# A ring layout of its own for the second expert pass, and the last pass's down projection cut into column pieces of 512, 384 and 128

## The reference

```python
def swiglu(h, w_gate, w_up, w_down):
    return (jax.nn.silu(h @ w_gate) * (h @ w_up)) @ w_down

def moe_swiglu(h, w_router, w_gate, w_up, w_down):
    ...
    out = jnp.zeros_like(t)
    for e in range(N_EXPERTS):
        out = out + combine[:, e:e + 1].astype(t.dtype) * swiglu(t, w_gate[e], w_up[e], w_down[e])
    return out.reshape(B, S, D)

# behind both layers
return rms_norm(x, final_norm_g)
```

## Time and profile before

| | us |
|---|---|
| median of 3 runs | 1017.01 |
| lowest, highest | 1016.84, 1018.2 |
| the profiled execution, its own time | 1018.07 |
| its span, first to last instruction | 1016.3 |

### The profile page before, as it was taken

How to read it: one execution, slowest core, us unless ns; L and a number is a source line. 1 busy time by engine, 2 the same in 40 slices (tenths; PEclk the granted TensorE clock), 3 DMA queues, 4 the chain that set the end, 5 groups by cost and what they waited for, 6 DMA issues and landing times.

```text
span 1016.3 us, 22250 instructions
## 1 busy us (share of the span) xinstructions
PE 1001.5 (99%) x9679; PEld 863.3 (85%) x9679; DVE 592.1 (58%) x991; ACT 401.6 (40%) x627; POOL 13.6 (1%) x57
## 2 busy tenths in 40 slices
PE   8999999999999999999999999999999999999995
PEld 8999999999999999999999999996566566566552
DVE  6667766577677565376577665755542542542443
ACT  6735655535544344357356565352102002002012
POOL 3000000000000000000000000000000000000000
PEclk9999999999999999999999999999999999999998
DMA  7453543555555465465435437989979999999993
GB/s 282 160 159 104 198 146 111 187 200 189 176 187 186 144 217 201 150 232 166 163 107 188 154 99 263 394 326 405 405 305 414 410 411 414 413 408 414 414 408 139
DMA packets 56017, 255.40 MB, mean 251 GB/s; under 512 B 6609, under 2 KB 6641, under 8 KB 55922
## 3 DMA queue, kind: packets, MB, share of 16 engines
q1 hardware_dynamic: 55346, 252.94, 67.2%
q10 hardware_dynamic: 576, 1.07, 0.3%
HBM read 252.93 MB, written 1.05 MB: 250 GB/s over the span
## 4 chain that ended last, share of the span: by engine, by line
PE 85%; SPq 9%; DMA 3%; issue 1%; ACT 1%; DVE 1%; DVEq 0%
PE ps L1721 24%; PE ps L1716 18%; PE ps L1717 18%; PE ps L1718 18%; SPq L611 8%; PE ps L1710 2%; PE ps L1711 2%; PE ps L1712 2%; DMA e_ring<-in_experts 2%; DMA raw<-in_dense 1%; PE ps L1926 1%; ACT w_hi L754 0%; ACT squared L759 0%; PE ps L1744 0%; PE ps L1898 0%
## 5 line engine op out<-in xcount | busy, mean ns | idle before, releaser
L1075 DVE TENSOR_TENSOR w_lo<-raw,w_hi 128x1536 fp32r<-128x1536 f32 (+2 forms) x156 | 247.5, 1605 | 122.0 <-ACT w_hi L754 121.6
L754 ACT ACTIVATE w_hi<-raw 128x1536 fp32r<-128x1536 f32 (+2 forms) x156 | 209.2, 1362 | 145.2 <-DMA raw<-in_dense 142.5
L1716 PE MATMUL ps<-hT_hi,w_hi 128*128 128x256 f32 (+1 forms) x816 | 231.7, 284 | 1.6 <-DVE w_lo L1217 1.1
L1717 PE MATMUL ps<-hT_lo,w_hi 128*128 128x256 f32 (+1 forms) x816 | 230.4, 282 | 0.0
L1718 PE MATMUL ps<-hT_hi,w_lo 128*128 128x256 f32 (+1 forms) x816 | 229.6, 281 | 0.0
L1721 PE MATMUL ps<-e_ring,xe 128*32 128x352 f32 (+2 forms) x2480 | 186.5, 459 | 0.0
L1721 PEld LDWEIGHTS ps<-e_ring,xe 128*32 128x32 f32 x2480 | 109.8, 110 | 73.0 <-issue 32.3
L1716 PEld LDWEIGHTS ps<-hT_hi,w_hi 128*128 128x128 f32 (+1 forms) x816 | 152.2, 186 | 5.2 <-issue 2.6
L1717 PEld LDWEIGHTS ps<-hT_lo,w_hi 128*128 128x128 f32 (+1 forms) x816 | 152.3, 187 | 0.4
L1718 PEld LDWEIGHTS ps<-hT_hi,w_lo 128*128 128x128 f32 (+1 forms) x816 | 152.3, 187 | 0.4
L1717 PE MATMUL ps<-h_lo,w_hi 128*128 128x256 f32 x352 | 99.2, 282 | 0.0
(11 more groups left out here) (313 smaller groups left out, 1427.9 us busy)
## 6 DMA issues: line engine op xcount, KB each, us to landing
e_ring<-in_experts SPq DMA_DIRECT2D x124, 704.0 KB, 15.6
raw<-in_dense SPq DMA_DIRECT2D x112, 768.0 KB, 4.3
e_ring<-in_experts SPq DMA_DIRECT2D x88, 512.0 KB, 14.5
raw<-in_dense SPq DMA_DIRECT2D x42, 512.0 KB, 3.5
e_ahead<-in_experts SPq DMA_DIRECT2D x4, 704.0 KB, 9.1
raw<-in_dense SPq DMA_DIRECT2D x3, 544.0 KB, 4.9
raw<-in_dense SPq DMA_DIRECT2D x2, 272.0 KB, 4.2
x<-in_x SPq DMA_DIRECT2D x2, 256.0 KB, 4.5
```

Source lines behind the costliest of these rows:

```text
L754: act.activation(slot(n, "hi", k), slot(n, "raw", k), ACT.Copy).then_inc(hi_done, 1)
L1075: dve.tensor_tensor(slot(n, "lo", k), slot(n, "raw", k), slot(n, "hi", k).bitcast(F32), ALU.subtract).then_inc(lo_done, 1)
L1716: pe.matmul(out, wh, hi, start=first, stop=False, skip_group_check=True)
L1717: pe.matmul(out, wh, lo, start=False, stop=False, skip_group_check=True)
```

## The change

**SP and the ring.** `e_first_place` and `e_first_before` now take the pass as well. Pass 0 keeps its places. Pass 1 has its own: units 0 to 2 go to the columns 0 to 4223 of the ring, which pass 0 leaves with its unit 23, 22 and 21; units 3 and 4 go to `e_ahead`; units 5 to 23 go to where units 0 to 18 were before; from unit 24 on, all have the places of before. The waits are worked out from the overlaps. The loads of pass 2 are written out too, since their waits follow from pass 1's places, and the loop begins at pass 3. The multiplications of passes 0 and 1 read from the new places.

**TensorE, ACT and DVE at the end of the last pass.** The 1024 output columns are cut at 512 and 896. For k = 0 to 7 the right half is multiplied on its first 384 columns only. For k = 8, 9, 10 only the left 512 columns are multiplied as each k lands; then come the overflow of the three, then the 384 columns of the three, then the last 128 columns for k = 0 to 2, then the scatter of the 512 and of the 384 columns, then the last 128 columns for k = 3 to 10, and their scatter. ACT makes `y_hi` of the left half before `weighted_over`; the 384 columns are split into `y_hi` and `y_lo`, as the left half is; DVE makes the last 128 columns (`ehid`) itself. The norm's squares have three pieces.

```diff
-LAST_BANKS = ((2, 3), (0, 1))
+LAST_BANKS = ((2, 3), (0, 1), (5, 7))
...
+LAST_CUT = HALF + 384
+NORM_PIECES = [[], [], [], OCOLS, [(0, HALF), (HALF, LAST_CUT - HALF), (LAST_CUT, D - LAST_CUT)]]
...
+def e_first_place(i, u):
+
+    gate_up, size = 4 * 2 * KQ, 2 * HALF_E
+    shift = len(AHEAD) * size // D
+    if i == 0 and u in AHEAD:
+        return "ahead" + str(AHEAD.index(u) // 2), AHEAD.index(u) % 2 * size, size
+    if i == 0 and 24 <= u < gate_up:
+        return ("ring",) + e_place(u - len(AHEAD))
+    if i == 0 and u >= gate_up:
+        at = CHUNK_AT[0] + size * (gate_up - len(AHEAD) - 24) + D * (u - gate_up)
+        return ("ring",) + ((at, D) if at + D <= CHUNK_AT[0] + CHUNK else e_place(u - shift))
+    spare = shift * D // size
+    if i == 1 and u < spare:
+        return "ring", e_place(len(E_UNITS) - 1)[0] + size * u, size
+    if i == 1 and u < spare + 2:
+        return "ahead0", (u - spare) * size, size
+    if i == 1 and u < 24:
+        return ("ring",) + e_place(u - spare - 2)
+    return ("ring",) + e_place(u)
+
+
+def e_first_before(i, u):
+
+    buffer, at, size = e_first_place(i, u)
+    out = 0
+    for j in range(i + 1):
+        for v in range(u if j == i else len(E_UNITS)):
+            other, a, n = e_first_place(j, v)
+            if buffer == other and a < at + size and at < a + n:
+                out = max(out, j * E_GROUPS + E_GROUP[v] + 1)
+    return out
...
-            for u in range(len(E_UNITS)):
-                sp.wait_ge(e_used, E_GROUP[e_first_before(u)] + 1 if u < 24 else E_GROUPS + E_GROUP[e_before(u)] + 1)
-                expert_load(u, experts)
-            with sp.Fori(2, iters) as i:
+            for i in range(1, 3):
+                experts = [sp.value_load(ids[0:1, 2 * i + e:2 * i + e + 1], min_val=0, max_val=NE - 1) for e in range(2)]
+                for u in range(len(E_UNITS)):
+                    sp.wait_ge(e_used, e_first_before(i, u))
+                    expert_load(u, experts, i)
+            with sp.Fori(3, iters) as i:
...
+            weighted(0)
+            act.wait_ge(y_filled, last * 2 + 2)
             weighted_over()
-            act.wait_ge(y_filled, last * 2 + 2)
-            weighted(0)
             act.wait_ge(y_filled, last * 2 + 3)
-            act.activation(ehid[:, 0:HALF], ps[:, 6, :], ACT.Copy, scale=slot_scale[:, 0:1]).then_inc(y_hi_ready, 1)
...
+            w = LAST_CUT - HALF
+            act.activation(y_hi[:, HALF:LAST_CUT], ps[:, 6, 0:w], ACT.Copy, scale=slot_scale[:, 0:1]).then_inc(y_hi_ready, 1)
...
+            dve.wait_ge(y_hi_ready, last * 4 + 4)
+            rest(1, LAST_CUT - HALF)
+            last_rows(0)
+            last_rows(1)
+            dve.wait_ge(y_filled, last * 2 + 4)
+            dve.tensor_scalar(ehid[:, 0:D - LAST_CUT], ps[:, 4, 0:D - LAST_CUT], slot_scale[:, 0:1], None, ALU.mult).then_inc(last_ready, 1)
+            last_rows(2)
...
-            for q in range(DQ - 1):
-                down(q, last)
-            k = FET - 1
-            down_ready(k, last)
-            down_over([k]).then_inc(y_filled, 1)
-            for h in range(2):
-                down_main(k, h)
...
+            for k in range(late, FET):
+                down_ready(k, last)
+                down_main(k, 0)
+            down_over(range(late, FET)).then_inc(y_filled, 1)
+            for k in range(late, FET):
+                down_main(k, 1, w=w)
...
+            down_last(range(3))
+            pe.wait_ge(y_split, last * 3 + 5)
+            for tt in range(TT):
+                scatter(2 * tt, LAST_BANKS[0][tt])
...
+            pe.wait_ge(y_split, last * 3 + 6)
+            for tt in range(TT):
+                scatter(2 * tt + 1, LAST_BANKS[1][tt], w)
+            down_last(range(3, FET))
+            pe.wait_ge(last_ready, 1)
```

More of the change, by code:

```diff
@@ L532, in load_of, with e_unit @@
             return loaded[n % RING], 16 * (n // RING + 1)
-        def e_unit(u, first=False):
+        def e_unit(u, turn=None):
             _, _, _, k, _, c = E_UNITS[u]
[L537 to L542, removed]
+            buffer, at, size = ("ring",) + e_place(u) if turn is None else e_first_place(turn, u)
+            home = {"ring": e_ring, "ahead0": e_ahead, "ahead1": eb["e_ahead2"]}[buffer]
+            return home[:, at:at + size].rearrange("p (k c) -> p k c", k=k)
         def proj_bank(n):
@@ L641, in _ @@
             for u in free_later["wo"] + AHEAD:
[L642 removed]
+                expert_load(u, (0, 1), 0)
             sp.wait_ge(aux_done, ROUTER_AUX + 1)
@@ L2084, in quads, with hidden @@
                 return ins
-            def hidden(half, q, i, first=False):
+            def hidden(half, q, i, turn=None):
                 u = (half * KQ + q) * 4
-                units = [e_unit(u + n, first) for n in range(4)]
+                units = [e_unit(u + n, turn) for n in range(4)]
                 ks = (2 * q, 2 * q + 1)
@@ L2149, in k_pair, with down @@
                 return range(2 * q, min(2 * q + 2, FET))
-            def down(q, i, first=False):
+            def down(q, i, turn=None):
                 for k in k_pair(q):
@@ L2190, in _, with full_pass @@
             pe.wait_ge(moe_zero, 1)
-            def full_pass(i, first=False):
-                first_half(i, first)
-                second_half(i, first)
+            def full_pass(i, turn=None):
+                first_half(i, turn)
+                second_half(i, turn)
                 for q in range(DQ):
-                    down(q, i, first)
+                    down(q, i, turn)
                 pe.wait_ge(sel_ready, i + 2)
@@ L2226, in _ @@
-            pe.wait_ge(y_hi_ready, last * 4 + 3)
-            for tt in range(TT):
-                out, tokens = last_rows(0, tt)
-                plain(out, selT[:, 0, tokens], y_hi[:, 0:HALF], start=False, stop=False)
+            w = LAST_CUT - HALF
+            late = FET - 3
+            for q in range(late // 2):
+                for k in k_pair(q):
+                    down_ready(k, last)
+                    if k == TURNED:
+                        pe.wait_ge(turn1_read, last * 2 + 1)
+                    down_main(k, 0)
+                    down_main(k, 1, w=w)
+                if q == TURNED // 2:
+                    pe.wait_ge(turn1_read, last * 2 + 2)
+                down_over(k_pair(q))
@@ new lines, in _, with down_last, last_piece @@
+            for k in range(late, FET):
+                down_ready(k, last)
+                down_main(k, 0)
+            down_over(range(late, FET)).then_inc(y_filled, 1)
+            for k in range(late, FET):
+                down_main(k, 1, w=w)
+            def down_last(ks):
+                for k in ks:
+                    down_main(k, 1, LAST_CUT, D - LAST_CUT, 4)
+            def last_piece(tt):
+                return ps[:, LAST_BANKS[2][tt], 0:D - LAST_CUT], slice(tt * P, (tt + 1) * P)
```

111 lines of the change are left out of this document (46 added, 65 removed).

## The result

| | before | changed |
|---|---|---|
| median of 4 runs, us | 1017.17 | 1025.34 |
| lowest, highest | 1016.84, 1018.2 | 1021.64, 1026.02 |
| the profiled execution | 1018.07 | 1021.64 |

The ratio is 1.0071, with a 95% interval of 1.0058 to 1.0083: slower, by more than the range on record allowed. The four executions of the changed kernel took 1021.64, 1025.08, 1025.59 and 1026.02 us, with mean granted clocks of 0.998, 0.996, 0.994 and 0.994. Only the first, which is also the profiled one, lies where the forecast had it. One later execution each of before (1675.8 us), e6 (1311.54) and e9 (5720.59) was in a slow state and is left out of all figures.

A forecast was written before the change was run, and what follows sets the result against it. The prediction took the last down block's landing, T = 1000.2 us, fed by full DMA engines, to set the end. Ring +0.4 and end +3.1 made +3.5 on 1017.0: 1020.5 us, range 1018.8 to 1022.8.

The forecast's parts named there:

- Slower: Whole kernel: time more than 0.2% above the kernel before; chance 0.80.
- the hole: Expert-pass transfers: DMA share lacks 6.5 us at 730 to 750 us; claimed to move from 740 to 782 us, not close.
- Part 2: End of the last pass: from last landing to norm's reduction grows from 9.1 to 12.2 us, +3.1 us.
- Part 1: Pass 1's ring: units 0 to 23 land 6.0 us earlier, the gain is lost, last landing moves by +0.4 us.
- the ring's +0.4: Pass 1's ring: last landing comes 0.4 us later, bounds -0.2 and +0.8.
- the landing of unit 27: Pass 1's ring: unit 27 waits for value 17, at 791.2, and lands at 795.3 us, against 794.9 before.
- rival 3: TensorE at the last down blocks: clock falls to half, work dearer by up to 4 us, 1022 to 1025; chance 0.10.
- Rival 1: Ring's 6.0 us kept: last landing at 994.2, 1014.1 us; decides from where it comes 3.1 us earlier; chance 0.08.
- The 4.5 us put off behind T: Last pass: overflow 0.9, 384 columns 1.3 and 128 columns 2.3 us, formerly done while data came in, follow the last landing.

The follow-up runs named there:

- e6: Kernel before, with pass 1's ring units laid so that none from 24 on waits late, and the old end: 1015.65 us, ratio 0.9986.
- e9: e6 with the places of units 24 and 30 of pass 1 exchanged, so unit 24 waits late again; old end: 1017.8 us, ratio 1.0011.
- e5: Changed kernel with pass 1's units from 24 on laid elsewhere, so that none waits late; new end kept: 1017.46 us, ratio 1.0003.
- e3: Kernel before with only the new end of the last pass, ring unchanged: 1019.82 us, ratio 1.0035.
- e2: Kernel before with only the new ring places of pass 1, old end: 1019.27 us, ratio 1.0024.
- e11: Changed kernel run again unaltered, to trace an execution with a lower clock: 1022.55 us, ratio 1.0055.
- e14: Changed kernel with three matmuls of unused product in each of the waits for k = 9 and 10: 1022.97 us, ratio 1.0060.
- e8: Kernel before with the new end's pieces, but nothing put off behind the landing of k = 10: 1020.49 us, ratio 1.0029.
- e1: Changed kernel run once more unaltered: 1022.76 us, ratio 1.0057 to the kernel before.
- e10: e8 with overflow ahead of the left half, y2 ahead of y_hi and y_lo, and ehid ahead of DVE's additions: 1018.2 us, ratio 1.0011.

## Why the prediction was wrong

**The direction and the mechanisms held.** Slower was given 0.80. The data set the end before and after; the hole went from 740 to 780 us and did not shrink (7.0 and 7.6 us of missing transfers), since TensorE finishes group 1 when it does, data or no data: counted from the issue of unit 53, the value 16 lets a load go 54.9 us later in before, in the changed kernel, in e9, and in e5, whose queue never ran dry there. Part 2, the longer end, was foretold at +3.1 us and measured at +3.2 in the trace and +2.9 in time (e3), with its steps right to 0.1 or 0.2 us.

**The step that failed first** is in Part 1: "So the landings are 0.4 us later than before from here on. From unit 31 on, the engines are full again". The term of the sum that was mis-sized is the ring's +0.4: it measured +1.9 us at the landing of unit 31 (the medians of nine traces and of five, counted from the issue of unit 53) and +2.4 in the median (e2), beyond its upper bound of +0.8. T - L53 alone would have said anything from +0.8 (e11) to +2.3 (e14). The working took the landing of unit 27 for the whole price of the second wait. It is not: with three units of 1.7 us in the queue and a next one that needs 4.3 us from issue to landing, transfers thin out at 790 to 794 us. Unit 27 is 0.7 us later than in before, and unit 30 is 2.1 us later. What had to be compared was the work that is queued at an issue, 1.6 us, with those 4.3 us; this says that a dent comes, and not how much it costs. e9, with the second wait gone, gives back 1.5 us and leaves 0.4.

**The second is rival 3**, the clock. It was given 0.10 and taken for a state that the kernel is in or not. A lower clock came in 7 of 18 executions, 3 of the 4 that made up the result. Its price was given as up to 4 us; it is 1.5 to 2.2 in the traces and 2.3 between the medians, in which the landings' spread is too. That waits of 1.46 us with the clock at 1.00 spoke against it was weak: there TensorE did 2.15 us of matmuls for every k (0.86 each for the two halves, 0.43 of overflow) and not 0.86. That it would *add* to whatever ring and end cost was missed, so the range had no place for all three together. What brings the fall in one execution and not in the next stays open.

**The sum.** 1017.0 + 1.9 (ring, at unit 31) + 3.2 (end, in the trace) makes 1022.1, and the 11 executions without a fall have a median of 1022.1. A fall puts 2.3 on top: 1024.4. The remaining 1 us to 1025.34 is not accounted for. That the profiled execution, 1021.64, is 1018.07 + 3.5 to a tenth is luck: the execution of before began its experts 1.2 us later, and this hid what the ring lost.

**Rival 1's point of decision stands.** It said that the change pays from where T comes 3.1 us earlier; in e5 it does by 3.2 to 3.4, and its ratio is 1.0003. The small part that rival 1 left out is that with the old end the same ring is faster still.

**Part 2's reading was half right.** The 4.5 us put off behind T are in the path only where ACT and DVE are not: taking nearly all of them away gives 1.6 us in the trace (e8) and nothing that the medians can tell. DVE's and ACT's small steps of 0.05 to 0.4 us behind the last sets stood in the sum without a row each; together they came out right to 0.2 us.

## What to carry to other kernels

When loads go to places that come free earlier, look at the whole chain of waits behind them, through the next pass too (e5 lost 3.1 us there), and compare at each wait the transfers still queued with the time from issue to landing: a queue of three units runs thin although TensorE doesn't wait. Give the next units the places that have long been free, so that the late wait comes when the queue is deep (e5). Work moved behind a last landing costs only what the slowest engine's chain doesn't cover, but the clock can fall in the waits ahead of it, in some executions and not in the one that was profiled: so look at every execution's clock, not at one trace. And when traces are compared, count from an issue ahead of the change: it scatters less than a landing.

## What the runs showed of the hardware

- The granted clock fell to 0.50 in the second of two waits of 1.46 and 1.45 us with 1.06 us of matmuls in between (e11), and stayed at 1.00 in other executions of the same kernel with waits of 1.45 and 1.45 us (the profiled one) and 1.44 and 1.45 us (e1).
- The engines don't run dry together: in the changed kernel, from 776 us to the last landing at 780.7, the share went 0.78, 0.16, 0.00.
- In one execution of e8 the clock also fell in the mixer, at 542.3 us, behind a wait of 1.8 us for ACT, which was splitting a weight that had landed late; its unit 53 landed at 741.7 us, where the other traces of this kernel and of e3 and e10 have 737.5 to 738.3.
